# Mixer front of a one-core inference step: gate projection before each tile's blocks, its scan chain inside the projection stage, input weights in five separate blocks

## What is computed

```python
h = rmsnorm(x, norm1_g) * (1 + mod[:, 1]) + mod[:, 0]
p = h @ w_in + b_in                       # 2576 columns: q, k, v, o (512 each), 16 gates, u (512)
# gates: input and forget gate of 4 heads, forward and backward
b = jnp.cumsum(jax.nn.log_sigmoid(f_pre))             # within a chunk of 128
w_log = g[..., None] - b + ig                         # g: the chunk's last b
m_loc = jnp.max(w_log, axis=-1)
...
m_new = jnp.maximum(g_c + m, m_l)                     # over the chunks
C_new = a[..., None, None] * C + bb[..., None, None] * C_l
...
u -> real part of a DFT over positions and channels (64 x 16 grid for the latent tokens)
x = x + mod[:, 2] * (concat(mLSTM heads, DFT) @ w_out)
h = rmsnorm(x, norm2_g) * (1 + mod[:, 4]) + mod[:, 3]
x = x + mod[:, 5] * expert_choice_moe(h)              # 16 experts
```

## Time and profile before

| what | value |
|---|---|
| median of three runs | 2382.61 us |
| the profiled execution: time, and span of its instructions | 2383.4 us, 2381.6 us |
| TensorE busy | 2193.2 us (92%) |
| VectorE, ScalarE, GpSimd busy | 491.8, 356.1, 269.0 us |
| mean granted TensorE clock | 0.966 |
| HBM traffic over the span | 222 GB/s |

### The profile page before, as it was taken

The page is one execution under the profiler, slowest core; times in us unless marked ns, Lnnn a source line. Parts: engine busy times, 40 slices in busy tenths (PEclk is TensorE's granted clock), DMA queues, the critical chain, the costliest instruction groups (busy, mean ns, idle before and its releaser), DMA issues. The chain is left out here.

```text
span 2381.6 us, 37032 instructions
## 1 busy us (share of the span) xinstructions
PE 2193.2 (92%) x15013; PEld 1894.9 (80%) x15013; DVE 491.8 (21%) x1249; ACT 356.1 (15%) x1011; POOL 269.0 (11%) x266
## 2 busy tenths in 40 slices
PE   5999999767997199999999999999999999999992
PEld 1445554565654099999999999999999999999992
DVE  0111111546774601011101110111111011101102
ACT  0111111412322001111111011111111110111102
POOL 0000000011121102021020120210211202202102
PEclk9999999898999599999999999999999999999996
DMA  9631010226431766897976977979879769779775
GB/s 376 245 108 62 31 62 22 94 91 224 149 103 62 225 234 204 295 305 230 350 240 246 363 219 260 346 223 316 280 238 365 219 247 363 220 281 321 226 258 178
DMA packets 351601, 528.76 MB, mean 222 GB/s; under 512 B 12996, under 2 KB 292284, under 8 KB 348232
## 3 DMA queue, kind: packets, MB, share of 16 engines
q1 hardware_dynamic: 336456, 509.35, 61.8%
q0 software_dynamic: 15104, 18.88, 3.8%
HBM read 492.23 MB, written 35.95 MB: 222 GB/s over the span
## 5 line engine op out<-in xcount | busy, mean ns | idle before, releaser
L1588 PE MATMUL ps_ab<-xeT,ring 128*128 128x144 f32 x8192 | 1007.9, 287 | 14.6 <-DVE xeT L1633 14.6
L1588 PEld LDWEIGHTS ps_ab<-xeT,ring 128*128 128x128 f32 x8192 | 1006.2, 191 | 14.7 <-issue 14.7
L1601 PE MATMUL ps_yy<-hidT,ring 128*128 128x144 f32 x4096 | 504.4, 287 | 0.0
L1601 PEld LDWEIGHTS ps_yy<-hidT,ring 128*128 128x128 f32 x4096 | 502.8, 191 | 0.0
L422 PE MATMUL ps_p<-w_in_sb,hT 128*128 128x512 f32 x720 | 320.2, 599 | 4.2 <-DMA w_in_sb<-in_w_in 4.2
L422 PEld LDWEIGHTS ps_p<-w_in_sb,hT 128*128 128x128 f32 x720 | 135.7, 193 | 158.9 <-issue 155.7
L1637 DVE TENSOR_TENSOR hidT<-silu,ps_ab 128x144 f32<-128x144 f32 x256 | 78.0, 305 | 885.6 <-ACT silu L1555 885.6
L1534 POOL DMA_INDIRECT stream<-ye,slot_row x64 | 100.9, 1577 | 1215.1 <-DVE ye_p L1648 1200.4
L1555 ACT ACTIVATE silu<-ps_ab 128x144 f32<-128x144 f32 x256 | 74.2, 290 | 908.8 <-PE ps_ab L1588 908.8
L1177 PE MATMUL b_z<-y,mixT 128*128 128x512 f32 x288 | 128.1, 598 | 10.2 <-ACT aff L1111 10.2
L1641 DVE STREAM_TRANSPOSE yS<-yT 128x1024 f32<-128x1024 f32 x16 | 19.9, 1246 | 457.2 <-ACT yT_p L1562 457.2
(11 more groups left out here) (250 smaller groups left out, 1096.4 us busy)
## 6 DMA issues: line engine op xcount, KB each, us to landing
ring<-in_exp_w SPq DMA_DIRECT2D x384, 1024.0 KB, 12.4
y<-in_ada_w SPq DMA_DIRECT2D x22, 1024.0 KB, 7.6
w_in_sb<-in_w_in SPq DMA_DIRECT2D x4, 2048.0 KB, 19.6
kv<-kvo SPq DMA_DIRECT2D x15, 512.0 KB, 5.8
kvo<-pr SPq DMA_DIRECT2D x9, 768.0 KB, 3.3
qkT_dram<-qkT SPq DMA_DIRECT2D x9, 512.0 KB, 4.4
qk<-qkT_dram SPq DMA_DIRECT2D x9, 512.0 KB, 5.0
m_in<-m_lanes SPq DMA_DIRECT2D x9, 512.0 KB, 5.8
```

The lines of the kernel that those rows point to most:

```text
L1588: mm = nc.tensor.matmul(ps_ab[f % 2][:, N * w:N * w + N], unit[:, k, bass.ts(c, P)], xeT[:, k], start=(k == 0), stop=(k == DT - 1))
L1601: mm = nc.tensor.matmul(ps_yy[d % 2][:, 0:N], unit[:, f % 2, bass.ts(d, P)], hT[:, f], start=(f == 0), stop=(f == FT - 1))
```

## The change

1. **Gates first.** From tile 1 on, PE does a tile's eight gate matmuls before its `block_sum(0)`; tile 0 keeps them at its end, and tile 1 begins by waiting until tile 0's gate rows have been kept. DVE adds the gate bias as it copies the gate rows, so the four additions at the end are gone.
2. **The chain in the last tile.** The chain is cut in four pieces that DVE runs in tile 8: `forget_start` before block 0 is kept, `forget_sums`, `forget_peaks`, `forget_exponents` after blocks 0, 1 and 2. ACT's two functions stand at the start of its tile 8, its three exponentials at the end. The 36 transposes, the carry matmuls and the copies to `g.cols` and `g.carry` stand at the end of `front`. The chain's rows lie in memory that is free by then (x, block 0 of `w_in`, half of `pr`).
3. **recurrence** has none of this left: ACT goes through its copies without the exponentials, PE goes from the DFT straight to the states, and PE's first wait is for `state_C` and `state_n` alone.
4. **Weights.** In SBUF each block of `w_in` is contiguous in its partition (`g.w_blocks[b]`), instead of a range of columns of one matrix. In the queue, block 1 comes ahead of `b_in_row`, blocks 2 and 3 ahead of x and the constants, and block 4 ahead of the constants; `b_gate` still follows all of them.

```diff
                 load_weights(0)
+                load_weights(1)
                 sp.dma_start(g.b_in_row[:], g.b_in.to_broadcast([P, IN_COLS])).then_inc(g.b_in_loaded, 16)
-                load_weights(1)
+                load_weights(2)
+                load_weights(3)
                 sp.dma_start(xt[:, 1], g.x_rows(1)).then_inc(x_loaded[1], 16)
+                load_weights(4)
                 sp.dma_start(g.const[:, P:], g.constants[:, P:]).then_inc(rest_loaded, 16)
-                for b in range(2, 5):
-                    load_weights(b)
+                sp.wait_ge(minus_half_set, 2)
...
@@ front, ScalarE, tile 8
+                        act.wait_ge(f_abs_ready, 1)
+                        g.act.did(nc.scalar.activation(t_row, t_row, ACT.Exp, scale=-1.0))
+                        g.act.settle()
+                        g.act.did(nc.scalar.activation(t_row, t_row, ACT.Ln, bias=1.0), soft_ready)
...
+                        act.wait_ge(exponents_ready, 3)
+                        for row, scale in ((wi_row, -1.0), (em_row, -1.0), (t_row, 1.0)):
+                            g.act.did(nc.scalar.activation(row, row, ACT.Exp, scale=scale), weights_ready)
@@ front, TensorE
+                    if only(i, 1):
+                        pe.wait_ge(gates_kept, 1)
...
-                            mm = nc.tensor.matmul(ps_p[(par + b) % 2][:], hT[:, par, k], g.w_in_sb[:, k, COLS[b]:COLS[b] + 512],
+                            mm = nc.tensor.matmul(ps_p[(par + b) % 2][:], hT[:, par, k], g.w_blocks[b][:, k, W_FROM[b]:W_FROM[b] + 512],
...
+                    if not only(i, 0):
+                        gate_sum()
                     block_sum(0)
...
+                pe.wait_ge(weights_ready, 3)
+                pe.wait_ge(qk_kept, 2 * TILES)
+                for q, row in enumerate((e_row, wi_row, em_row, t_row)):
+                    for i in range(TILES):
+                        mm = nc.tensor.transpose(ps_cols[q][:, NR * i:NR * i + NR], row[0:NR, bass.ts(i, P)], g.ident[0:NR, 0:NR])
+                    mm.then_inc(cols_turned, 1)
@@ front, VectorE
+                    def keep_gates():
+                        dve.wait_ge(gates_summed, i + 1)
+                        g.dve.did(nc.vector.tensor_scalar(g.gate_rows[:, bass.ts(i, P)], ps_g[:, 0:P], b_gate[:, 0:1], None, ALU.add), gates_kept)
+                    if not only(i, 0):
+                        keep_gates()
+                    if last:
+                        forget_start()
...
+                        if last:
+                            (forget_sums, forget_peaks, forget_exponents, nothing, nothing)[b]()
...
+                keep_cols()
                 g.dve.settle()
-                for j in range(4):
-                    s = slice(32 * j, 32 * j + HEADS)
-                    g.dve.did(nc.vector.tensor_scalar(g.gate_rows[s, :], g.gate_rows[s, :], b_gate[s, :], None, ALU.add))
-                g.dve.settle()
@@ recurrence, ScalarE
-                    if n == 12:
-
-                        act.wait_ge(exponents_ready, 3)
-                        for row, scale in ((wi_row, -1.0), (em_row, -1.0), (t_row, 1.0)):
-                            did(nc.scalar.activation(row[:], row[:], ACT.Exp, scale=scale), weights_ready)
@@ recurrence, TensorE
-                pe.wait_ge(init_loaded, 64)
+                pe.wait_ge(start_loaded, 32)
```

More of the change, by code:

```diff
@@ L456, in body @@
                         pe.wait_ge(weights_set, 1)
-                    pe.wait_ge(qk_kept, 2 * i + 2)
-                    for k in range(DT):
-                        mm = nc.tensor.matmul(ps_g[:, 0:P], w_gate[:, k], hT[:, par, k], start=(k == 0), stop=(k == DT - 1))
-                    mm.then_inc(gates_summed, 1)
+                        gate_sum()
                 def dft_cols(i, par, j):
@@ L488, in _ @@
                 dft_cols(TILES - 1, 0, 1)
+                pe.wait_ge(weights_ready, 3)
[4 more added lines that the diff above has]
+                    mm.then_inc(cols_turned, 1)
+                pe.wait_ge(wi_last_ready, 1)
+                pe.wait_ge(gate_kept, 4)
+                for r in range(LANES):
+                    mm = nc.tensor.matmul(ps_ada[:, TILES * r:TILES * r + TILES], g.pick_lane[0:64, bass.ts(r, P)], wi_last[:], start=True, stop=True)
+                mm.then_inc(carry_spread, 1)
             @block.vector
@@ new lines, in forget_peaks @@
+                def forget_peaks():
+                    did(TT(e_row, g.gate_rows[0:64, :], b_row, ALU.subtract))
+                    settle()
+                    dve.wait_ge(gates_summed, TILES)
+                    did(SCAN(g.m_row[FWD, :], keep[FWD, :], e_row[FWD, :], 0.0, ALU.add, ALU.max))
+                    did(SCAN(g.m_row[BWD, ::-1], keep[BWD, ::-1], e_row[BWD, ::-1], 0.0, ALU.add, ALU.max))
+                    settle()
+                    for rows, at in ((FWD, P - 1), (BWD, 0)):
+                        did(COPY(b_last[rows, :], chunks(b_row[rows, :])[:, :, at]))
+                        did(COPY(e_last[rows, :], chunks(g.m_row[rows, :])[:, :, at]))
+                    dve.wait_ge(init_loaded, 32)
+                    settle()
@@ new lines, in keep_cols @@
+                def keep_cols():
+                    dve.wait_ge(weights_ready, 3)
+                    for rows, at in ((FWD, P - 1), (BWD, 0)):
+                        did(COPY(wi_last[rows, :], chunks(wi_row[rows, :])[:, :, at]), wi_last_ready if at == 0 else None)
+                    for q in range(4):
+                        dve.wait_ge(cols_turned, q + 1)
+                        src = ps_cols[q][:, 0:NR * TILES].rearrange("p (n c) -> p n c", c=NR)
+                        for d in range(2):
+                            did(TS(g.cols[:, q, :, HEADS * d:HEADS * d + HEADS], src[:, :, 32 * d:32 * d + HEADS],
+                                   K_SCALE if q == 3 else 1.0, None, ALU.mult))
+                    dve.wait_ge(carry_spread, 1)
+                    did(COPY(g.carry[:], ps_ada[:, 0:LANES * TILES].rearrange("p (r n) -> p r n", n=TILES)))
@@ L554, in _ @@
                 g.dve.did(nc.vector.memset(g.minus_half[:], -0.5), minus_half_set)
+                g.dve.did(nc.vector.memset(b_gate[:], 0.0), minus_half_set)
                 g.dve.did(nc.vector.memset(w_gate[:], 0.0))
@@ L636, in _ @@
             def _(sp):
-                sp.dma_start(c_init[:], g.state_C.rearrange("(r v) k -> v r k", v=HD)).then_inc(init_loaded, 16)
-                sp.dma_start(n_init[:], g.state_n).then_inc(init_loaded, 16)
-                sp.wait_ge(m_init_zeroed, 1)
-                with nc.allow_non_contiguous_dma("one stabiliser per partition"):
-                    for d in range(2):
-                        sp.dma_start(m_init[32 * d:32 * d + HEADS, :], g.state_m[HEADS * d:HEADS * d + HEADS, :]).then_inc(init_loaded, 16)
+                sp.dma_start(c_init[:], g.state_C.rearrange("(r v) k -> v r k", v=HD)).then_inc(start_loaded, 16)
+                sp.dma_start(n_init[:], g.state_n).then_inc(start_loaded, 16)
                 def load(n):
@@ L868, in _ @@
-                dve.wait_ge(carry_spread, 1)
-                did(nc.vector.tensor_copy(carry[:], bk[2][:, 0:LANES * TILES].rearrange("p (r n) -> p r n", n=TILES)), carry_kept)
                 settle()
```

218 lines of the change are left out of this document (105 added, 113 removed).

## The result

The changed kernel takes 2372.96 us (median of five runs, 2369.28 to 2373.61); the kernel before, beside it on the same chip, 2384.6 us. The ratio is 0.9945, interval 0.9934 to 0.9957: shorter, as forecast, and by more than the 0.2% that the prediction set as the least to be told. That is 11.6 us by the medians. The profiled execution took 2370.94 us with a span of 2369.1, 12.5 less than the span before; the sum of the prediction was 11.3 less.

What follows compares the result with a forecast made beforehand. TensorE, busy 92% of the span, was taken as the bound, so only its idle or low-clock time in the first 530 us counted. 0.6 + 4.6 - 0.7 - 8.1 - 6.0 - 1.7 = -11.3 us, giving 2371.3 us, range 2367.5 to 2377.

Steps and rivals of the forecast that it cites:

- Bound and first tile: TensorE busy 92%; in the first tile VectorE still waits for `b_gate`, so the weights' order and layout bring 0.
- Rival 2: First tile: the start gets shorter, the idle 13.6 us goes, -24 us in all, 2358 us; chance 0.04.
- Gates first, +0.6: Tile 1: the gate sum newly waits until tile 0's gate rows are kept, +0.6 us (0.4 to 0.8).
- The chain fits: Tile 8: the chain fits VectorE's idle time with 0.6 us to spare, cost 0; keeps may be some 7 us late.
- rival 3: Tile 8: the chain does not fit; slower from about 1.75 times its durations, 2389 us at twice; chance 0.02.
- End of `front`, +4.6 - 0.7: Transposes and carry matmuls moved behind the last DFT matmul add 4.6 us; the block closing sooner after TensorE saves 0.7.
- Rival 1: Lower clock in the thin matmuls ending `front` or in the first states: about -7, 2375.5 us; chance 0.14.
- Start of `recurrence`, 0: Without the wait for `state_m`, `state_C` still lands at nearly the same time: 0, at best -2.4 us.
- DFT, -8.1: DFT of `recurrence` without ScalarE's exponentials: the 6.24 us wait and the slower matmuls behind it go, -8.1 us.
- After the DFT, -6.0: First states start sooner after the DFT: 4.6 us of work moved to `front` and 1.4 us of waiting gone.
- the first sums, -1.7: First eight state sums in `recurrence` run at the upper clock right behind the DFT: -1.7 us (bounds 0 and -1.8).
- Rival 4: Little happens: the removed stall is taken over elsewhere in `recurrence`, for instance by key loads; about 2379 us, chance 0.06.

Runs made afterwards that it cites:

- run 3: Kernel before with only the weights' part: `w_in` in five contiguous blocks and the changed queue order; 2385.27 us, ratio 1.0003 to the kernel before.
- run 1: Changed kernel with the four `b_gate` transfers issued right behind tile 0 of x, ahead of all of `w_in`; 2356.07 us, ratio 0.9886 to the kernel before.
- run 6: Kernel before with only the gates' part: gate matmuls ahead of the blocks from tile 1, bias added in the copy; 2384.68 us, ratio 0.9999.
- run 7: Changed kernel with each of the chain's four scans done twice in tile 8; 2381.47 us, ratio 0.9993 to the kernel before.
- run 4: Kernel before, with TensorE at the start of `recurrence` waiting only for `state_C` and `state_n`, not `state_m`; 2383.93 us, ratio 0.9997.
- run 8: Changed kernel with 36 transposes and eight 9-column matmuls, results unused, put back before the first states; 2378.18 us, ratio 0.9972 to the kernel before.
- Run 5: Kernel before with ScalarE's three exponentials taken one each after DFT copies 18, 21 and 24, instead of all after copy 12; 2375.96 us, ratio 0.9963.

## Why the prediction was right, point by point

- **Bound and first tile: right.** `b_gate` held VectorE and through it TensorE; run 3 measures the 0 (ratio 1.0003), run 1 removes the cause. Rival 2 gave that idle time 13 us; it did not come with this change, as said, but it is there: 15.0 us in run 1.
- **Gates first, +0.6: right.** The wait is 0.65 us in the changed kernel and in run 6. The +0.5 at the end of `front` is a net figure and meets it in part by luck: 0.4 us less in tile 0 and 0.25 more at the end of tile 8 nearly cancel.
- **The chain fits: right in what it said of the result, wrong in the margin.** "A keep may be some 7 us late" looked at VectorE and TensorE only; of ScalarE the prediction reckoned that the exponentials are there before the columns want them at 431.4, and not that ScalarE's own copy for the DFT, wanted near 430, stands behind them. Run 7 shows that ScalarE's order gives out first, at about 4 us, and that a stall there costs a second time through the clock. 10.5 us more of VectorE's work, on the 26.3 that the prediction gives the chain, took nearly the whole gain away, so by this run the point at which rival 3 turns into a loss, "about 1.75 times", is nearer 1.4 (an estimate: the work was added to two of the four pieces only).
- **End of `front`, +4.6 - 0.7: right.** Measured +4.8 - 0.7. The clock fell at 435.2, 1.5 us before the end of the carry factors, where before it fell at 497.4, 1.1 us before it: that is the 0.2. Rival 1, which had it low all through or in the first states, did not happen. The earlier trace rows gave the right size without saying why, and run 1, where these matmuls keep the upper level to their end, shows that when the fall comes was worth up to 0.7 us: to that extent the hit was luck.
- **Start of `recurrence`, 0: off by 0.9.** The step that failed is "`state_C` lands at nearly the same time". The reason given for it held (run 4: `state_m` costs nothing), but TensorE's start itself varies between 4.4 and 5.5 us after the first load. The instruction packet goes with it in all eleven traces; that it is the cause was not shown. It was within the bound of -2.4.
- **DFT, -8.1: right.** From the third pair on 40.04 us instead of 48.14. The further 0.6 at its start was not in the sum: the low stretch ends at 445.4, 3.4 us into the matmuls, and before at 442.8, 4.5 us into them, and 1.1 us less at half the clock is the 0.6. Runs 1 and 8, with the same code there, have 5.0 us of it, so this gain does not come in every execution. Run 5 shows how little of this step's gain needs the chain gone.
- **After the DFT, -6.0, and the first sums, -1.7: right.** -6.1 and -1.8. Run 8 gives back 1.0 of the latter with thin matmuls alone, so their place before the sums explains at least that much; the other 0.8 is not separated by any run.
- **Nothing after 530 us: right.** 1845.3 us in both. Rival 4 did not happen: from VectorE's first copy of the states to the first matmul behind them it takes 25.2 us (490.75 to 515.98), as before (503.71 to 528.95), so VectorE still sets its pace, and the loads of keys moved along.

The clock deserves a paragraph of its own. In run 8 TensorE was busy 5.00 of 5.00 us before 494 and 2.00 of 2.00 after, and the clock fell at 495.2; in the changed kernel it fell within the carry factors, at 2.60 of 2.60. The Trainium skill, "TensorE: Matmul & The Clock Gate", Part 1, ties the gate to how busy the engine was; taken by the busy time of the rows, the runs contradict that for 36- and 9-column matmuls. The same page, Part 4, adds that transposes do not count as busy in the same way, and with that the traces agree: 36 transposes stand ahead of each of these falls, the last of them 0.9 us before the fall in the changed kernel and 2.6 us before it in run 8. Whether the transposes or the thin matmuls behind them are the cause no run here separates.

## What to carry to other kernels

A wait's length is set by the transfer that lands last, so look what a first consumer waits for and put the smallest such transfers first: here four tiny ones cost 11.5 us in the kernel before and 15 in the changed one, about what the whole change brought, and made a better order of the large ones look worthless. Reckon the margin of moved work on every engine that has a piece of it, in that engine's own order, not only on the one that does most. And before moving a chain to another block, try to split the burst that stalls: three exponentials behind a late chain, all in one place, cost 8 us here, spread out about one.

## What was unexpected of the hardware

- The clock fell with TensorE fully busy, behind transposes and thin matmuls (0.79, then 0.50 in run 8), and in run 7 it stayed at 0.50 for 20.5 us around short stalls and the wait for `state_C`, twice as long as the low stretch at that place in the kernel before or after (10.2 us each).
- From the issue of `state_C`, the same 512 KB at the same place, it took from 4.4 to 5.5 us until TensorE started; the six slower traces had one instruction packet beside it, the five faster ones none.
- What is won early does not all arrive: run 1 is 17.7 us ahead of after at the first load of `recurrence`, 16.4 at the first matmul of `mixing` and 15.0 at the end. Of the first 1.3 us lost 0.8 are the DFT's longer stretch at the lower clock; the last 1.4 are the difference of 1846.7 and 1845.3 us behind the start of `mixing`, and their cause stays open.
